# Router on unnormalised rows, first expert pair gathered in fp32 from the accumulator, one memset and three loads moved

## The reference, cut to what matters

```python
h = x + m @ w_out
hn = h * rsqrt(mean(h * h) + EPS) * g_ffn
logits = hn @ w_router + b_router
vals, idx = lax.top_k(logits, 4)
probs = softmax(vals)
for e in range(32):
    g = minimum(hn @ w_gate[e] + b_gate[e], 7.0)
    u = clip(hn @ w_up[e] + b_up[e], -7.0, 7.0)
    hdn = (u + 1.0) * (g * sigmoid(1.702 * g))
    out = out + combine[:, e:e + 1] * (hdn @ w_down[e] + b_down[e])
y = rmsnorm(h + out, g_final)
```

## Time and profile before

| | |
|---|---|
| median of 3 runs | 1195.98 us (1195.93 to 1196.72) |
| the profiled execution | 1196.15 us |
| its span, as the trace has it | 1194.4 us |
| mean granted clock of TensorE | 0.993 |
| busy share of the span: TensorE matmuls, VectorE, ScalarE, GpSimd | 93%, 36%, 14%, 8% |
| moved by DMA | 440.38 MB, mean 369 GB/s |

### The profile page before, as it was taken

One profiled execution on the slowest core, in us unless ns is written; L12 is line 12 of the kernel. 1 busy time (PEld: TensorE's weight loads), 2 busy tenths in 40 slices (PEclk: granted clock), 3 DMA queues, 4 the chain that ended last, 5 costly groups with the idle time before them and its releaser, 6 DMA issues.

```text
span 1194.4 us, 15234 instructions
## 1 busy us (share of the span) xinstructions
PE 1110.8 (93%) x5769; PEld 509.0 (43%) x5770; DVE 429.0 (36%) x1012; ACT 166.4 (14%) x329; POOL 90.6 (8%) x124
## 2 busy tenths in 40 slices
PE   6999999989999989899999898999999999999896
PEld 5777777654433324233433232333333333333333
DVE  4899999442132313131222222222222121212123
ACT  3211156230010010101000000000000000000103
POOL 3565220130000000000000000000000000000000
PEclk9999999989999999999999999999999999999999
DMA  9973433559999999999999999999999999999995
GB/s 285 318 232 135 152 136 109 212 193 374 427 428 426 426 429 427 427 427 427 427 429 430 427 427 429 430 429 427 427 429 430 428 428 428 429 430 427 429 427 191
DMA packets 59298, 440.38 MB, mean 369 GB/s; under 512 B 4983, under 2 KB 27767, under 8 KB 34795
## 3 DMA queue, kind: packets, MB, share of 16 engines
q1 hardware_dynamic: 58042, 436.94, 89.2%
q0 software_dynamic: 1024, 2.77, 0.8%
q10 hardware_dynamic: 192, 0.14, 0.0%
HBM read 438.24 MB, written 2.43 MB: 369 GB/s over the span
## 4 chain that ended last, share of the span: by engine, by line
PE 70%; DMA 27%; DVE 1%; ACT 1%; issue 0%; SPq 0%; DVEq 0%
PE ps L1149 26%; DMA ring<-in_w_gate 24%; PE ps L941 13%; PE ps L1209 11%; PE ps L1239 4%; PE ps L1128 4%; PE ps L1029 3%; PE ps L1052 2%; DMA ring<-in_w_down 2%; PE ps L909 2%; PE ps L1141 1%; PE ps L1243 1%; PE ps L1019 1%; PE ps L1334 1%; PE ps L1130 1%; PE ps L1202 1%
## 5 line engine op out<-in xcount | busy, mean ns | idle before, releaser
L1149 PE MATMUL ps<-ring,ws 128*64 128x512 f32 x2032 | 460.6, 598 | 40.7 <-DMA ring<-in_w_up 24.5
L1149 PEld LDWEIGHTS ps<-ring,ws 128*64 128x64 f32 x2032 | 139.6, 137 | 329.8 <-issue 247.8
L1209 PE MATMUL ps<-ring,ws 128*64 128x512 f32 x960 | 216.7, 595 | 6.9 <-DMA ring<-in_w_down 6.9
L941 PE MATMUL ps<-ws,ring 128*128 128x288 f32 x640 | 158.6, 410 | 0.0
L941 PEld LDWEIGHTS ps<-ws,ring 128*128 128x128 f32 x640 | 122.7, 192 | 34.2
L1209 PEld LDWEIGHTS ps<-ring,ws 128*64 128x64 f32 x960 | 65.7, 137 | 125.5 <-issue 105.5
L1712 DVE TENSOR_TENSOR acc<-ps,acc 128x1024 f32<-128x1024 f32 x30 | 36.8, 1225 | 191.6 <-PE ps L1239 191.6
L1689 DVE TENSOR_SCALAR ws<-ps 128x512 f32<-128x512 f32 x32 | 22.1, 692 | 197.2 <-PE ps L1149 197.2
L1508 DVE SCALAR_TENSOR_TENSOR ps<-ws,par,ps 128x256 f32<-128x256 f32 x232 | 91.8, 483 | 0.2 <-DVE ps L1508 0.2
L1694 DVE TENSOR_SCALAR ws<-ps 128x512 f32<-128x512 f32 x32 | 22.1, 692 | 159.5 <-PE ps L1149 159.5
L813 ACT COPY ws<-ps 64x512 f32<-64x512 f32 x62 | 35.9, 579 | 257.8 <-PE ps L1209 257.5
(11 more groups left out here) (228 smaller groups left out, 699.0 us busy)
## 6 DMA issues: line engine op xcount, KB each, us to landing
ring<-in_w_up SPq DMA_DIRECT2D x64, 2048.0 KB, 25.0
ring<-in_w_gate SPq DMA_DIRECT2D x63, 2048.0 KB, 24.9
ring<-in_w_down SPq DMA_DIRECT2D x60, 2048.0 KB, 23.7
ring<-in_w_in SPq DMA_DIRECT2D x20, 1024.0 KB, 13.4
ring<-in_w_conf_pw SPq DMA_DIRECT2D x4, 1024.0 KB, 6.0
ring<-in_w_out SPq DMA_DIRECT2D x4, 1024.0 KB, 6.1
ring<-in_w_down SPq DMA_DIRECT2D x4, 1024.0 KB, 22.7
ws<-in_w_gate SPq DMA_DIRECT2D x2, 1024.0 KB, 16.4
```

Of the source, the lines that this page charges most:

```text
L941: ins = nc.tensor.matmul(z[:, 0:T], w[:, k, i * P:(i + 1) * P], hn[:, k, :], start=(k == 0), stop=(k == NT - 1))
L1149: ins = nc.tensor.matmul(ps[h * CAP:(h + 1) * CAP, bk + q // 2, :], x_e[:, KQ * (q % 2) + t, b, :], w[:, t, h * 512:(h + 1) * 512], start= ...
L1209: ins = nc.tensor.matmul(ps[h * CAP:(h + 1) * CAP, bk, :], hid_t[:, b, k % KQ, k // KQ, :], w[:, h * 512:(h + 1) * 512], start=False, stop ...
```

## The change

- **Memset.** GpSimd's memset of `bias` waits until VectorE has emptied `hn7`, the last turned tile of x.
- **Loads.** `early_down[3]` is issued after `early_down[1]`, and the 2 MB into `spare` after chunk (0,2), when `gb7` is filled and the recurrence has finished (`s_hs`). `h_tok` is now used only at the end.
- **Raw rows.** `turn_h` turns `acc` itself as soon as a half is complete; there is no `norm`. The gain is multiplied into `w_rt` once. The row factor (`h_factor`) is applied to the logits in `choose`. For the sample tile VectorE repeats the 32 rows of `acc` twice (`repeat_samples`).
- **A new wait.** Since `h_rest` takes the place of `st_h`, VectorE waits before `complete(2)` until all stored output rows have landed (`s_store`).
- **Order on TensorE.** The turning of tile 0 comes before `out10`; the first half of tile 1 is turned in the middle of `out11`, and the second half between the two halves of `logits1`. The squares of tile 1 are summed in halves.
- **Smaller router tail.** The mask is made in bf16 at once, ranks count from 1, and the sample rows of the mask are bounded by using 32 rows (`tri_s`) in place of clearing and copying.
- **First pair.** `gather_first` gathers experts 0 and 1 together in fp32 from `acc`, with selections that carry the row factor (`sel_inv`), 24 fp32 matmuls of 128 columns in two banks. `gather(0, 0)` and `gather(1, 1)` are gone, and so are the two `take_inputs` of 64 slots.
- **Parts.** ScalarE makes the high part from `acc` with the factor and the middle part; VectorE makes the rest (`rest`) and the low part (`low`). GpSimd does none of it. The parts are first waited for at the gather for experts 2 and 3.

```diff
-    jobs += [(n, "v") for n in ("out2", "out00", "ht2a", "ht2b", "out01", "logits2", "out10", "ht0a", "ht0b", "out11",
-                                "logits0", "ht1a", "ht1b", "logits1", "rank")]
+    jobs += [(n, "v") for n in ("out2", "out00", "ht2a", "ht2b", "out01", "logits2", "ht0a", "ht0b", "out10", "logits0",
+                                "ht1a", "out11", "ht1b", "logits1", "rank")]
...
+        h_rest = hid_t_w[:, 0:D]
...
                 sp.wait_ge(filled, JOB["i7"] + 1)
                 for k in range(2):
+                    load_early(k)
+                sp.wait_ge(s_st, N_ST)
+                load_early(3)
                 load_gu(0, 2)
+                sp.wait_ge(filled, JOB["gb7"] + 1)
+                sp.wait_ge(s_hs, 1)
+                for h in range(2):
+                    sp.dma_start(spare[:, h * HALF:(h + 1) * HALF],
+                                 w_down[EARLY, 1, :, h * HALF:(h + 1) * HALF]).then_inc(s_early, 16)
                 load_gu(0, 3)
                 load_gu(1, 0)
...
                 sp.wait_ge(filled, JOB["logits1"] + 1)
                 load_early(2)
-                sp.wait_ge(s_split, 3 * TILES)
-                for h in range(2):
-                    sp.dma_start(spare[:, h * HALF:(h + 1) * HALF],
-                                 w_down[EARLY, 1, :, h * HALF:(h + 1) * HALF]).then_inc(s_early, 16)
                 load_gu(1, 3)
...
+                pool.wait_ge(empt_v, EV("hn7"))
                 pool.memset(bias[:, :, :], 0.0)
...
-                for n, i in enumerate(TILE_ORDER):
-                    rest(n, i)
...
                 out_rows(0, (0,))
-                turn_h(2)
+                for h in range(2):
+                    turn_h(2, h, (s_rep, 1))
                 out_rows(0, (1,))
                 logits(2)
+                for h in range(2):
+                    turn_h(0, h, (empt_v, EV(f"out0{h}")))
                 out_rows(1, (0,))
-                turn_h(0)
-                out_rows(1, (1,))
                 logits(0)
-                turn_h(1)
-                logits(1)
+                fill("ht1a")
+                z = fill("out11")
+                for k in range(NT):
+                    if k == NT // 2:
+                        turn_h(1, 0, (empt_v, EV("out10")))
+                    ins = nc.tensor.matmul(z[:, :], mt[:, k, P:2 * P], w_out_cols(k, 1), start=(k == 0), stop=(k == NT - 1))
+                ins.then_inc(filled, 1)
+                fill("ht1b")
+                z = fill("logits1")
+                logits_half(1, 0, z)
+                turn_h(1, 1, (empt_v, EV("out11")))
+                logits_half(1, 1, z).then_inc(filled, 1)
...
+                def gather_first(z, ts):
+
+                    for n, t in enumerate(ts):
+                        for i in range(TILES):
+                            rows = P if i < 2 else T_S
+                            ins = nc.tensor.matmul(z[:, n * 2 * CAP:(n + 1) * 2 * CAP], acc[0:rows, i, cols(t)],
+                                                   sel_inv[0:rows, i].rearrange("p b s -> p (b s)"),
+                                                   start=(i == 0), stop=(i == TILES - 1))
+                    return ins
...
-                gather(0, 0)
+                pe.wait_ge(s_selp, TILES)
+                for h, bk in ((1, BK_X), (0, BK_SEL)):
+                    gather_first(ps[:, bk, :], range(4 * h, 4 * h + 4)).then_inc(s_xg, 1)
                 pe.wait_ge(empt_v, EV("rank"))
...
+                V.tensor_tensor(w_rt[:], w_rt[:], g_ffn[:, :].unsqueeze(2).to_broadcast([P, NT, E]), ALU.mult)
+                V.tensor_copy(tri_s[0:T_S, :].rearrange("p (g t) -> p g t", g=4),
+                              tri[0:T_S, 0:T_S].unsqueeze(1).to_broadcast([T_S, 4, T_S]))
+                dve.wait_ge(s_store, N_STORES)
                 complete(2)
-                norm(2)
+                repeat_samples()
                 complete(0, (0,))
-                take_turned(2)
+                mean_square(2, TILES + 1, 12)
+                h_factor(0, 2)
+                for h in range(2):
+                    take_turned(2, h)
+                rest(0, 2)
...
                 link(V.scalar_tensor_tensor(rank[:, :, :], zr, 1.0, mask_h[:, :, :], ALU.add, ALU.mult))
-                link(V.tensor_scalar(rank[:, :, :], rank[:, :, :], -1.0, None, ALU.add))
-                for r in range(1, 3):
-                    ins = V.tensor_copy(rank[r * T_S:(r + 1) * T_S, 2, :], rank[0:T_S, 2, :])
-                link(ins)
+                for i in range(TILES):
+                    for b in range(2):
+                        ins = V.tensor_scalar(sel_inv[:, i, b, :], slot_no[:, :], rank[:, i, b:b + 1], stat[:, 21 + i:22 + i],
+                                              ALU.is_equal, ALU.mult)
+                    ins.then_inc(s_selp, 1)
```

More of the change, by code:

```diff
@@ L1265, in _ @@
                 pe.wait_ge(s_xe, 1)
-                for q in range(1, 4):
+                gate_up_chunk(0, 1, slots[0], fills[0], last=False)
+                pe.wait_ge(s_xe, 2)
+                for q in range(2, 4):
                     gate_up_chunk(0, q, slots[q - 1], fills[q - 1], last=(q == 3))
-                gather(1, 1)
                 for m in range(2):
                     gate_up_bias(1, 1, m, BK_OUT)
-                pe.wait_ge(s_xe, 2)
                 gate_up_chunk(1, 0, slots[3], fills[3], BK_OUT)
@@ new lines, in h_factor, with take_turned, h_rows_of @@
+                def h_factor(n, i):
+                    dve.wait_ge(s_root, TILES + n + 2)
+                    V.reciprocal(stat[:, 21 + i:22 + i], stat[:, 18 + i:19 + i]).then_inc(s_hn, 1)
+                def take_turned(i, h):
+                    z = full(f"ht{i}{'ab'[h]}")[:, :].rearrange("p (k t) -> p k t", k=4)
+                    V.tensor_copy(h_cm[:, 4 * h:4 * h + 4, i * P:(i + 1) * P], z).then_inc(empt_v, 1)
+                def h_rows_of(i, s):
+                    rows = P if i < 2 else (3 - s) * T_S
+                    return rows, (h_split[:, s, i, :] if i < 2 else h_rows[0:rows, :])
@@ new lines, in rest, with low @@
+                def rest(n, i):
+                    dve.wait_ge(s_split, 2 * n + 1)
+                    rows = h_rows_of(i, 1)[0]
+                    high = h_split[:, 0, i, :] if i < 2 else h_rows[0:rows, :]
+                    V.scalar_tensor_tensor(h_rest[0:rows, :], acc[0:rows, i, :], stat[0:rows, 21 + i:22 + i], high, ALU.mult,
+                                           ALU.subtract).then_inc(s_rest, 1)
+                def low(n, i):
+                    dve.wait_ge(s_split, 2 * n + 2)
+                    rows, part = h_rows_of(i, 2)
+                    mid = h_split[:, 1, i, :] if i < 2 else h_rows[0:rows, :]
+                    V.tensor_tensor(part, h_rest[0:rows, :], mid, ALU.subtract).then_inc(s_low, 1)
@@ L1627, in _ @@
+                for h in range(2):
+                    take_turned(0, h)
                 complete(1, (0,))
-                take_turned(0)
+                choose(1, 0)
+                rest(1, 0)
+                take_turned(1, 0)
+                low(1, 0)
                 complete(1, (1,))
-                norm(1)
-                choose(0)
-                take_turned(1)
-                choose(1)
+                take_turned(1, 1)
+                dve.wait_ge(s_sq, 2 * TILES)
+                V.tensor_scalar(stat[:, 16:17], stat[:, 13:14], stat[:, 9:10], D * EPS, ALU.add, ALU.add).then_inc(s_ms, 1)
@@ L1744, in _ @@
                 link(ins)
[L1746 removed]
+                low(2, 1)
                 clamp_gate(0, None)
```

172 lines of the change are left out of this document (91 added, 81 removed).

## The result

The kernel with the change takes **1203.89 us** (median of 5 runs, 1201.74 to 1204.86), against 1196.58 us (1195.93 to 1197.93, 5 runs) for the kernel before on the same chip: a ratio of 1.0059, 95% interval 1.0048 to 1.007. It is slower by 7.3 us. The forecast was 1194.3 us, and the range ended at 1197.3 us. The profiled execution took 1203.93 us; its span is 1202.2 us, its mean granted clock 0.986.

What follows compares the result with a forecast made beforehand. Bound: a full-rate weight stream whose start hangs on TensorE's chain. First slot 1.1 us earlier plus 0.6 us of closed hole, 1.7 us off 1196.15 us, gave 1194.45 us, forecast as median 1194.3 us; range 1191.4 to 1197.3 us.

Steps and rivals of the forecast that it cites:

- What bounds the kernel: From about 280 us a full-rate weight stream; its start, SyncE's first load waiting for a freed ring slot (274.99 us), sets the end.
- The loads: Early weight loads: moving them alone brings nothing, cost and gain 0, with a bound of 0.5 us either way.
- The memset: Start of the kernel: moving GpSimd's memset brings VectorE's factors 2.3 us earlier; with 0.6 us from TensorE's pace, 2.9 us.
- the second term: TensorE's first matmuls, 16.57 to 21.0 us: with less idle time ahead, the pace may double sooner, gaining 0.6 us.
- The new wait: VectorE waits for GpSimd's second store, landing 7.3 us after issue, before adding sample rows; `out01` and all behind 1.5 us later.
- rival D: The stores land late, 16.4 us after issue, delaying everything queued behind: 9.1 us more, 1203.4 us; chance 0.06.
- Router and tail: Tile 2's turning to the gather: last logits end at 261.5 us, 2.1 us gained; then 3.7 us to the gather's start.
- The gather: First pair's 24 fp32 matmuls, 48 instructions: 5.2 us at 2.4 GHz, 10.3 us at 1.2 GHz, taken as 7.3 us.
- The clock: TensorE's clock falls before the first pair's gather and returns inside it after some 4.3 us, costing 2.1 us.
- rival B: The clock does not fall, or returns before the gather, which takes 5.2 us: 1192.2 us, or 1191.4 us; chance 0.30.
- The hole: A gap of 0.6 us in the DMA stream at 296 to 298 us, expected to close as later slots come sooner.

Runs made afterwards that it cites:

- the mixture: Changed kernel with first-pair tiles 2 and 0 gathered from bf16 parts, only tile 1 in fp32, store wait later: 1191.9 us, ratio 0.9964 against the kernel before.

## Why the prediction was wrong

- **What bounds the kernel: right.** The end is the issue of that load plus a constant.
- **The loads: right**, cost and gain nothing, as far as the run with the loads put back tests it.
- **The memset: right in kind, a little too large.** Forecast 2.3 + 0.6 = 2.9 us; the mixer ran 2.45 us earlier (`w_conf_pw` at 184.58 us, before at 187.03). The factors gave 2.03 of it, the shorter L941 0.74, and the first piece of `w_in` took 0.32 back (10.51 us, before 10.19). So the second term came to 0.4 us, but not by the pace doubling sooner after the first matmul. The memset alone gave 2.3 us by the ratio (0.0019 x 1196.5), 2.9 between the profiled executions.
- **The new wait: right in kind, somewhat too large.** 1.5 us forecast; TensorE stands idle 0.91 us for it, and the run without it gives 1.1 us by the traces, 1.5 by the medians. The second store landed 6.7 us after its issue, not 7.3, which is the difference; rival D is out. That the turning of tile 2 still came as forecast (228.51 us against 231.6 - 2.9 = 228.7) is luck: this wait was 0.6 us shorter than forecast, and the start gained 0.45 us less. By the Trainium skill (page "SBUF — State Buffer", section "SBUF: two separate sides") GpSimd's descriptors wait while VectorE runs a two-port operation such as an fp32 copy. Neither of the two small operations is one (a multiplication of two tensors and a bf16 copy), so that they could delay the landing was more than the page's sentence says. This trace does not test that: they ended at 217.86 us, before the first store was issued at 218.04 us.
- **Router and tail: right.** From the turning to the last logits it was 30.2 us, 29.9 forecast, and then 3.9 to the gather, 3.7 forecast. The gather started 0.34 us later than forecast.
- **The gather: this step failed.** It said "0.43 us each, so 0.107 us for 128: 5.2 us at 2.4 GHz, 10.3 us at 1.2 GHz. These are the two ends", and took 7.3 us. It was 15.99 us, beyond both. Two things were missing, which make up the 8.69 us: 4.14 and 4.55. First, an instruction of 128 columns does not cost a quarter of one of 512: it is 0.238 us at either clock, 11.44 us for 48. The working left the weight load out. Under an instruction of 512 columns (0.43 us, L1066) a load of the same form shows 0.19 us and then 0.24 us of pause; in the gather with 128 rows the loads have no pause. That suggests that this gather goes at the pace of its loads. What makes 0.24 us is open: the columns alone do not, the clock alone does not, and the stride was tried at a granted clock of 0.50 only. The nearest row stood in the earlier trace rows: six fp32 instructions of 128 columns, over the same three tiles, in 1.78 us, 0.30 us each, which gives 14.2 us. I used that row for its idle time and not for its pace. But it would have come so near in part by luck: in the sixteen traces here these six take 1.78 us in nine and 1.04 us (0.17 each, 8.3 us for 48) in seven, the change among them. Second, 15 changes between 128 and 32 rows at 0.30 us: 4.55 us. The loads of the change, of the six at the start and under 512 columns:

```profile
10.79 0.93 PEld L941 LDWEIGHTS ps<-ws,ones 128*128 128x128 f32 x6 [1.16 <-DVE ws L1477]
...
230.43 0.19 PEld L1066 LDWEIGHTS ps<-ring,ws 128*128 128x128 f32 x1 [0.24 <-issue]
```

  The six read adjacent columns. At 0.17 us each, with the step to 32 rows among them and no pause, they were quicker than any instruction of the fp32 gather. So adjacent columns at the full clock may cost less than 0.24 us, and a change of height less than here; no run gathers that way.
- **The clock, the other half of that step and rival B: wrong.** I let it return inside the gather after 4.3 us. It stayed at 0.50 for all of it, which the gather itself hardly felt, though I had charged it half of the time; the bias matmuls and the first chunk did feel it, 1.5 us.
- **The hole: it closed, but was sized too small.** 0.6 us forecast, 1.4 us measured (919.4 against 918.0). I read it from the DMA share (0.77). By the bytes in the same row, 254 GB/s where the stream has 428, it is 0.8 us, and the next window has 385 GB/s, 0.2 us more:

```profile
298.00:300.00 2.00, 2.00 (x12) 0.72 (x10) 0.00 (x0) 0.00 (x0) 0.00 (x0) 1.00 0.93 385
```

  The last 0.4 us are open.

The sum closes, as it must, being cut from the same two traces. From the gather's start to the load the forecast had 273.9 - 262.3 = 11.6 us; it was 284.19 - 262.64 = 21.55, 9.95 more: 8.69 in the gather, 0.19 up to the first chunk, 1.07 in the first chunk. With 0.34 us for the start and less 0.8 for the hole that is 9.5 us, and 1194.45 + 9.5 = 1203.95 us against the profiled 1203.93.

## What to carry to other kernels

Do not scale a matmul's time by its columns below the point where its weight load is hidden; take the price from rows of the same shape, type and rows, and from more than one: the only such row here, six instructions long, would have warned me, but it ran at 0.30 us in one execution and at 0.17 in another. Read a hole in the stream by its bytes, not by the busy share. A cheaper looking fp32 operand of 32 rows between others of 128 can cost more than it saves: pad it with zeros, or put the short ones together. And where work must wait for one late input, let only that part take the expensive route, as the mixture does.

## What the hardware showed that I had not expected

- Changing the stationary operand of fp32 matmuls between 128 and 32 rows cost 0.25 to 0.30 us each time (15.99 against 11.44 us with 15 changes; 12.18 us with 3), about 0.2 us each where the clock was 1.00 (22 instructions with 7 changes in 6.62 us, against 0.238 each). Among the six instructions at the start, when they took 1.04 us, one such change left no pause at all.
- The pace of the gather with 128 rows throughout did not follow the clock: about ten instructions in 2 us at 0.50 and at 1.00.
- 16 us of unbroken work with 32-row instructions among it left the granted clock at 0.50; half of the columns (14.28 us) and adjacent columns (15.03 us) did the same. With 128 rows throughout it was back after 3.8 to 5.6 us (four runs), and in the run with the short ones last it came back and fell again. A busy TensorE does not settle the clock; what does here is open.
- A memset of GpSimd stretched a VectorE operation from 0.29 to 3.26 us.
